# Norms at a stage's start: who builds the spreading matrix, where root's table is loaded, who splits the first weights, and in which order the first products run

## The reference

```python
def rmsnorm(x, g):
    y = xf * lax.rsqrt(jnp.mean(xf * xf, axis=-1, keepdims=True) + EPS)
    return y * g
def modulate(x, g, shift, scale):
    return rmsnorm(x, g) * (1 + scale) + shift
# first block, layers 0 and 1
a = modulate(h, norm1_g[l], sh1, sc1)          # gating MLP + differential attention, then window attention
h = h + g1 * mixer(a)
h = h + g2 * swiglu(modulate(h, norm2_g[l], sh2, sc2), ffn_w_in[l], ffn_w_out[l])
# then rmsnorm(h, final_g); second block, layers 0 and 1, with layer norms
x = layer_norm(ALPHA * x + g_m * y, ln_g[i, 0], ln_b[i, 0])
h = x * (1.0 + sc_f) + sh_f
x = layer_norm(ALPHA * x + g_f * swiglu_2(h, ...), ln_g[i, 1], ln_b[i, 1])
```

## Time and profile before

| | |
|---|---|
| runs | 4267.31 us median of 3 (4243.4 to 4297.15) |
| profiled execution | 4287.69 us, span 4285.9 us, mean granted clock 0.909 |
| TensorE | matmuls 3965.7 us (93%), 32782 |
| VectorE | 1375.1 us (32%), 2736 |
| ScalarE | 1225.9 us (29%), 2118 |
| GpSimd | 1268.8 us (30%), 669 |
| DMA | 343.5 MB, mean 80 GB/s |

### The profile page before, as it was taken

The page is one execution under the profiler, slowest core; times in us unless marked ns, Lnnn a source line. Parts: engine busy times, 40 slices in busy tenths (PEclk is TensorE's granted clock), DMA queues, the critical chain, the costliest instruction groups (busy, mean ns, idle before and its releaser), DMA issues. The chain is left out here.

```text
span 4285.9 us, 77448 instructions
## 1 busy us (share of the span) xinstructions
PE 3965.7 (93%) x32782; PEld 3303.3 (77%) x32782; DVE 1375.1 (32%) x2736; ACT 1225.9 (29%) x2118; POOL 1268.8 (30%) x669
## 2 busy tenths in 40 slices
PE   7988899999989999979699999889999989998997
PEld 5776788888777677758588988778888868766886
DVE  2327211111444211165455555432111140443112
ACT  1215211111345322232233333222111132543222
POOL 0211222222324343322122222222222222553442
PEclk6999999999999999989777677799999989998998
DMA  8210232232200434322201000113223211112222
GB/s 303 65 34 11 89 110 92 89 117 82 76 9 31 152 127 158 127 98 109 74 20 24 24 24 26 42 59 118 106 91 118 84 55 59 36 36 79 98 83 74
DMA packets 119177, 343.50 MB, mean 80 GB/s; under 512 B 34031, under 2 KB 40559, under 8 KB 118511
## 3 DMA queue, kind: packets, MB, share of 16 engines
q1 hardware_dynamic: 118895, 339.40, 23.0%
HBM read 324.55 MB, written 16.93 MB: 80 GB/s over the span
## 5 line engine op out<-in xcount | busy, mean ns | idle before, releaser
L204 POOL TENSOR_TENSOR feed_low<-ring,feed_high 128x1024 fp32r<-128x1024 f32 (+1 forms) x240 | 627.4, 2615 | 1375.7 <-ACT feed_high L197 1281.7
L221 PE MATMUL ps<-hn_high,feed_high 128*128 128x512 f32 (+1 forms) x2112 | 760.5, 360 | 24.1 <-DVE hn_low L827 13.8
L221 PE MATMUL ps<-hn_low,feed_high 128*128 128x512 f32 (+1 forms) x2112 | 753.1, 357 | 0.0
L221 PE MATMUL ps<-hn_high,feed_low 128*128 128x512 f32 (+1 forms) x2112 | 751.8, 356 | 0.0
L221 PEld LDWEIGHTS ps<-hn_high,feed_high 128*128 128x128 f32 x2112 | 402.1, 190 | 111.9 <-issue 23.4
L221 PEld LDWEIGHTS ps<-hn_high,feed_low 128*128 128x128 f32 x2112 | 401.9, 190 | 57.2
L221 PEld LDWEIGHTS ps<-hn_low,feed_high 128*128 128x128 f32 x2112 | 402.5, 191 | 54.9
L1298 DVE TENSOR_TENSOR ps<-feed_gate,ps 128x768 f32<-128x768 f32 (+1 forms) x88 | 73.0, 829 | 1009.9 <-PE ps L221 1009.1
L197 ACT ACTIVATE feed_high<-ring 128x1024 fp32r<-128x1024 f32 (+1 forms) x240 | 272.7, 1138 | 378.8 <-PE ps L221 378.8
L221 PE MATMUL ps<-feed_hid_high,feed_high 128*128 128x512 f32 (+1 forms) x1056 | 380.7, 360 | 0.0
L221 PE MATMUL ps<-feed_hid_low,feed_high 128*128 128x512 f32 (+1 forms) x1056 | 377.4, 357 | 0.0
(11 more groups left out here) (530 smaller groups left out, 7505.1 us busy)
## 6 DMA issues: line engine op xcount, KB each, us to landing
feed_side_ring<-in_ada SPq DMA_DIRECT2D x144, 512.0 KB, 5.8
ring<-in_ffn_g SPq DMA_DIRECT2D x88, 512.0 KB, 3.5
ring<-in_ffn_u SPq DMA_DIRECT2D x88, 512.0 KB, 3.5
ring<-in_ffn_d SPq DMA_DIRECT2D x64, 704.0 KB, 4.1
ring<-in_ada SPq DMA_DIRECT2D x48, 512.0 KB, 5.2
ring<-in_od_in SPq DMA_DIRECT2D x24, 512.0 KB, 3.4
ring<-in_ev_in SPq DMA_DIRECT2D x23, 512.0 KB, 4.4
ring<-in_even_in SPq DMA_DIRECT2D x20, 512.0 KB, 3.6
```

The lines of the kernel that those rows point to most:

```text
L204: pool.tensor_tensor(self.low[:, j % self.slots, 0:w], feed.ring[:, slot, 0:w], self.high[:, j % self.slots, 0:w].bitcast(F32), ALU.subtra ...
L221: mm = pe.matmul(dst, weights[a], values[b], start=first and n == 0, stop=last and n == 2)
```

## The change

`pick` is written by ScalarE with five copies, announced by a semaphore that TensorE waits for before a spread: ahead of the squares in stages with a mean, behind the root in those without. VectorE begins with the mean or the factor. Gains and shifts (`prepare`) are computed between the factor and the wait for the root. A square root of a constant is issued in the second half of the feed forward and in the output projection, one stage ahead of the norms. The low part of the first weight tile is written by VectorE, behind the root's split and before the scaling; GpSimd writes that of the second. `early_products` runs two passes for each step: high x high for all tiles as soon as the chunk's high part is there, then the two products with a low part.

```diff
--- before.py
+++ after.py
@@ -602,7 +602,6 @@
                     dve.wait_ge(turned, g - 1)
                 dve.tensor_copy(rows[:, g % 2, :], acc[:, g % 2, :]).then_inc(rows_copied, 1)
                 if g == KC:
-                    norm.sums.build(dve)
                     dve.wait_ge(sums.summed, KC)
                     norm.factor(dve)
             dve.wait_ge(turned, GROUPS)
@@ -670,16 +669,17 @@
 
     def __init__(self, k, st, tokens):
         self.k, self.n, self.q = k, tokens, tokens // 4
-        self.pick = st.sb("pick", [P, 4, P], F32R)
+        self.pick, self.picks_ready = st.sb("pick", [P, 4, P], F32R), st.sem("picks_ready")
         self.factor = st.sb("factor", [P, self.q])
         self.high, self.low = st.sb("factor_high", [P, self.q], F32R), st.sb("factor_low", [P, self.q], F32R)
 
-    def build(self, dve):
-        dve.tensor_scalar(self.pick[:, :, :], self.k.ones[:, :].unsqueeze(1).to_broadcast([P, 4, P]), 0.0, None, ALU.mult)
-        dve.drain()
+    def build(self, act):
+        act.activation(self.pick[:, :, :], self.k.ones[:, :].unsqueeze(1).to_broadcast([P, 4, P]), ACT.Copy, scale=0.0)
+        act.drain()
         for i in range(4):
             rows = slice(32 * i, 32 * i + 32)
-            dve.tensor_scalar(self.pick[rows, i, :], self.k.ones[rows, :], 1.0 / 32, None, ALU.mult)
+            ins = act.activation(self.pick[rows, i, :], self.k.ones[rows, :], ACT.Copy, scale=1.0 / 32)
+        ins.then_inc(self.picks_ready, 1)
 
     def add(self, pe, bank, values, first, last):
         return quarter_sums(self.k, pe, bank, values, self.q, first, last)
@@ -694,6 +694,7 @@
         return dve.tensor_tensor(self.low[:, :], self.factor[:, :], self.high[:, :].bitcast(F32), ALU.subtract)
 
     def spread(self, pe, dst):
+        pe.wait_ge(self.picks_ready, 1)
         for i in range(4):
             edges = [self.q * i] + [e for e in (512,) if self.q * i < e < self.q * (i + 1)] + [self.q * (i + 1)]
             for a, b in zip(edges, edges[1:]):
@@ -784,8 +785,11 @@
 
     def scalar(self, act):
         if self.offset is not None:
+            self.sums.build(act)
             self.squares(act)
         self.roots(act)
+        if self.offset is None:
+            self.sums.build(act)
 
     def roots(self, act):
         act.wait_ge(self.var_ready, 1)
@@ -850,23 +854,25 @@
         for c in range(KC):
             dve.tensor_tensor(self.k.h[:, c, 0:n], self.k.h[:, c, 0:n], self.root, ALU.add).then_inc(self.centred, 1)
 
-    def vector(self, dve):
-        if not self.rooted:
-            self.sums.build(dve)
-            if self.offset is not None:
-                self.centre(dve)
-            else:
-                self.factor(dve)
-        self.prepare(dve)
+    def vector(self, dve, weights=None):
+
         if self.offset is not None:
+            self.centre(dve)
             dve.wait_ge(self.summed, KC)
-            self.factor(dve)
+        if self.rooted:
+            self.prepare(dve)
+        else:
+            self.factor(dve, self.prepare)
+        if weights:
+            weights()
         self.apply(dve)
 
-    def factor(self, dve):
+    def factor(self, dve, meanwhile=None):
 
         sums = self.sums
         dve.tensor_scalar(sums.factor[:, :], sums.total(self.bank), 1.0 / D, EPS, ALU.mult, ALU.add).then_inc(self.var_ready, 1)
+        if meanwhile:
+            meanwhile(dve)
         dve.wait_ge(self.root_ready, 1)
         dve.reciprocal(sums.factor[:, :], sums.factor[:, :])
         sums.split(dve).then_inc(self.split_ready, 1)
@@ -938,18 +944,29 @@
 
     LAG = 2
     for step in range(KC + LAG * (len(tiles) - 1)):
-        if step < KC:
-            norm.wait(pe, step)
-        for n, (e, dst, tokens) in enumerate(tiles):
-            c = step - LAG * n
-            if not 0 <= c < KC:
-                continue
-            slot, cols = split.wait(pe, 0, e) if c == 0 else e % split.slots, slice(c * P, (c + 1) * P)
-            for a, b, _ in spans(tokens):
-                mm = split.products_of(pe, dst[:, a:b], (split.high[:, slot, cols], split.low[:, slot, cols]),
-                                       (k.hn[0][:, c, a:b], k.hn[1][:, c, a:b]), c == 0, c == KC - 1)
-            if c == KC - 1:
-                mm.then_inc(split.products, 1)
+        for low in range(2):
+            if step < KC and low:
+                norm.wait(pe, step)
+            elif step < KC:
+                pe.wait_ge(norm.high_ready, step + 1)
+            for n, (e, dst, tokens) in enumerate(tiles):
+                c = step - LAG * n
+                if not 0 <= c < KC:
+                    continue
+                if c == 0 and low:
+                    split.wait(pe, 0, e)
+                elif c == 0:
+                    pe.wait_ge(split.high_ready, e + 1)
+                slot, cols = e % split.slots, slice(c * P, (c + 1) * P)
+                for a, b, _ in spans(tokens):
+                    high, values = split.high[:, slot, cols], k.hn[0][:, c, a:b]
+                    if low:
+                        pe.matmul(dst[:, a:b], split.low[:, slot, cols], values, start=False, stop=False)
+                        mm = pe.matmul(dst[:, a:b], high, k.hn[1][:, c, a:b], start=False, stop=c == KC - 1)
+                    else:
+                        pe.matmul(dst[:, a:b], high, values, start=c == 0, stop=False)
+                if c == KC - 1 and low:
+                    mm.then_inc(split.products, 1)
 
 
 def layer_norm(k, tokens, which, bank):
@@ -979,6 +996,7 @@
 
         @st.block.scalar
         def _(act):
+            sums.build(act)
             for c in range(KC):
                 act.wait_ge(centred, c + 1)
                 if c >= 4:
@@ -992,7 +1010,6 @@
 
         @st.block.vector
         def _(dve):
-            sums.build(dve)
             dve.tensor_scalar(sums.factor[:, :], sums.total(bank), -1.0 / D, None, ALU.mult)
             sums.split(dve).then_inc(mean_split, 1)
             dve.wait_ge(mean_spread, 1)
@@ -1052,7 +1069,7 @@
 
 
     with ExitStack() as k.tmp, Stage(k, "project") as st:
-        split = Split(k, st, 2)
+        split, table = Split(k, st, 2), st.sb("table", [P, 1])
         mixed = st.sb("mixed_high", [P, KC, tokens], F32R), st.sb("mixed_low", [P, KC, tokens], F32R)
         high_ready, low_ready = st.sem("mixed_high_ready"), st.sem("mixed_low_ready")
         updated, restored = st.sem("stream_updated"), st.sem("stream_restored")
@@ -1079,6 +1096,7 @@
                 act.activation(mixed[0][:, c, :], k.mo[:, c, 0:tokens], ACT.Copy).then_inc(high_ready, 1)
                 if c == 1:
                     split.write_high(act, 0, 1)
+            act.activation(table[:, :], k.eps[:, 0:1], ACT.Sqrt)
             for n in range(KC):
                 if n + 2 < KC:
                     split.write_high(act, (n + 2) // 4, (n + 2) % 4)
@@ -1134,7 +1152,7 @@
     feed, side = k.feed, k.side
     FIRST, UP, DOWN = 2, 4 * (HALF // 2), 8
     with ExitStack() as k.tmp, Stage(k, "feed") as st:
-        split = Split(k, st, 2, SLOT)
+        split, table = Split(k, st, 2, SLOT), st.sb("table", [P, 1])
         with ExitStack() as front:
             rest, k.tmp = k.tmp, front
             norm = stream(st)
@@ -1179,7 +1197,7 @@
                     else:
                         if e == 0:
                             norm.after_split(pool)
-                        for j in range(2):
+                        for j in range(0 if e else 1, 2):
                             split.write_low(pool, 0, j, e)
                         if e == 0:
                             norm.gpsimd(pool)
@@ -1278,6 +1296,8 @@
                 feed.at = down
                 split.write_high(act, 0, 0, e2)
                 store_high(HALF - 1)
+                if h:
+                    act.activation(table[:, :], k.eps[:, 0:1], ACT.Sqrt)
                 for n in range(DOWN):
                     if n + 1 < DOWN:
                         split.write_high(act, (n + 1) // 4, (n + 1) % 4, e2)
@@ -1304,7 +1324,7 @@
 
                 feed.at, side.at = first, side_base + 2 * h
                 if h == 0:
-                    norm.vector(dve)
+                    norm.vector(dve, lambda: split.write_low(dve, 0, 0))
                     if next_c:
                         sm.products.vector(dve)
                 chunk(0, 0, 0, e)
@@ -1387,8 +1407,7 @@
             st.clear_last(pool)
             if norm:
                 norm.after_split(pool)
-                for e in range(2):
-                    split.write_low(pool, 0, e)
+                split.write_low(pool, 0, 1)
                 norm.gpsimd(pool)
             for e in range(2 if norm else 1, at):
                 split.write_low(pool, 0, e)
@@ -2239,7 +2258,6 @@
         def _(pool):
             st.clear_last(pool)
             norm.after_split(pool)
-            split.write_low(pool, 0, 0)
             split.write_low(pool, 0, 1)
             norm.gpsimd(pool)
             pool.memset(pads[0][:, :, :], 0.0)
```

## The result

The changed kernel takes **4235.6 us** (median of 19 runs, 4230.4 to 4248.6) against 4266.8 for the kernel before (19 runs, 4243.4 to 4297.2): ratio **0.9937, 95% interval 0.9921 to 0.9953**. That is 31 us of medians, where 13.5 were summed and 4254 forecast. It is 0.6%, so "same" by the forecast's line of 2%, though the interval is clear of 1. The lowest times differ by 13.0 us; over all runs on record (130 of the kernel before, 25 of the changed one) the lowest are 4238.1 and 4230.4 us, 7.8 apart. What shrank most is the scatter, from 54 to 18 us. The profiled execution took 4234.7 us with a span of 4232.9.

What follows compares the result with a forecast made beforehand. TensorE, busy 93% of the span, was taken to bound the kernel, so only its waits at normalising stages' starts could matter. Stage gains summed to 13.5 us: 4267.3 - 13.5 = 4254 us, range 4225 to 4286.

Steps and rivals of the forecast that it cites:

- Step 1: Four plain mean-square stages: matrix build leaves VectorE's path, 1.43 us won each; ScalarE's build takes 1.6, at most 0.4 lost in 512-token stages.
- Step 2: ScalarE's first-weight copies behind the matrix: no cost in wide stages, 0.25 us lost in 512-token ones; GpSimd done by about 6.3.
- Step 3 with 4: Layer-norm streams: gains and shifts in the root's wait cost 0.4 us each; root's table loaded a stage ahead wins 0.2 in three stages.
- Step 5: Four stages with a mean: VectorE takes the mean first, spread starts earlier, 0.8 us won each, between 0.3 and 1.4.
- Step 6: VectorE's first low part in the fourth feed forward no longer runs under GpSimd's weight operations: 1.0 us won; second feed forward nothing.
- Step 7: Early products, high parts first: TensorE does high products while low parts are awaited; 0.7 us per wide stage, 0.3 in 512-token feed forwards.
- The sum of waits: Gains of eight normalising stages added together: 13.5 us, 0.3%, between 6 and 22 with all bounds.
- The clock stays down: Rival: new pauses at early chunks delay the rise to 2.4 GHz; 4277 us, chance 0.13; milder form 4262, chance 0.22.
- GpSimd takes the weights first: Rival: in wide layer-norm stages GpSimd's weight split shuts out VectorE's, scaling 1.1 us late in two stages; 4256 us, chance 0.10.
- Lora's wait goes: Rival: a small shift lets VectorE's 5.30 us last-chunk operation go ahead of GpSimd, 3.4 us more won; 4251 us, chance 0.10.
- Loads come back: Rival: compiler loads root's table again at the stage, 0.2 us less in three stages, 1.3 in up to three; 4258, chance 0.05.

Runs made afterwards that it cites:

- experiment 9: Kernel before with only a delay: GpSimd does its first weight subtraction three times ahead of the recurrent stage; 4253.4 us, ratio 0.9975.
- part 1 alone: Kernel before with only the spreading matrix written by ScalarE instead of VectorE; 4245.3 us, ratio 0.9959.
- experiment 4: Changed kernel with high parts first undone, so each chunk's low products wait together with its high ones; 4248.6 us, ratio 0.9962.
- experiment 6: Kernel before with only the low part of the first weights moved from GpSimd to VectorE; 4246.0 us, ratio 0.9960.

## Why the prediction was right, and where it was short

The direction and the small size were right, the number 18 us too high. The measured time lies in the range by luck in part: the range had been widened by a scatter that I took for one of the measurement. By its steps:

- **Step 1** (matrix to ScalarE): removed as said. ScalarE's build took 1.94 us, not 1.6, for its narrow copies take 1.26 us together. In the wide stages it is still covered. In the second feed forward (below) and in lora the spread waited for it and not for the split; in the former it came 0.3 us after the split's end, inside the bound of 0.4.
```profile
1401.74 0.30 PE L702 MATMUL ps<-feed_factor_high,feed_pick 128*128 128x128 f32 x1 [3.28 <-ACT feed_pick L681]
```
- **Step 2** (copies behind it): VectorE's split ended 4.2 us after the root, before the spread (4.7); GpSimd 6.4 us after it (6.3 said). Right.
- **Step 3 with 4** (preparing, table): the loads are gone, and the inversion comes 0.91 us after the factor in the fourth feed forward against 0.88 before: the two cancel, where I had them at 0.2 lost and said 1.2 us.
```profile
3821.50 0.29 DVE L873 TENSOR_SCALAR feed_factor<-ps 128x128 f32<-128x128 f32 x1 [1.44 <-PE ps L637]
...
3822.41 0.94 DVE L877 RECIPROCAL feed_factor<-feed_factor 128x128 f32<-128x128 f32 x1
```
- **Step 5** (mean first): the spread starts 1.96 us after VectorE's first instruction against 2.45 and 2.61 before, so 0.5 to 0.65 us, not 0.8; ScalarE's longer build ends it.
```profile
3811.25 0.29 DVE L851 TENSOR_SCALAR feed_factor<-ps 128x128 f32<-128x128 f32 x1 [1.14 <-PEq L97]
...
3813.21 0.45 PE L702 MATMUL ps<-feed_factor_high,feed_pick 128*128 128x128 f32 x1 [2.61 <-ACT feed_pick L681]
```
- **Step 6** (first low part in the fourth feed forward): 1.70 to 0.75 us, as said. But the stage's end moved only 0.3 us of the 1.9 summed. Its lead of 2.8 us at the gate tile's SiLU (26.6 us after the spread of the mean, 29.4 before) is given back in the middle, with TensorE busy throughout at a granted clock of 1.00: 265 matmuls in 60 us before, 259 after. What slows them was not settled. Before, then after:
```profile
4004.00:4064.00 60.00, 60.00 (x265) 49.48 (x265) 6.64 (x9) 13.09 (x11) 26.36 (x9) 1.00 0.34 120
```
```profile
3953.00:4013.00 60.00, 60.00 (x259) 48.07 (x258) 6.65 (x9) 11.22 (x9) 26.57 (x9) 1.00 0.30 103
```
- **Step 7** (high parts first) is the mis-sized term: 0.7 and 0.3 us a stage, 4.1 together, measured 13 alone and 13 undone. Of these some 5 are waits outside lora (3.4 summed there), 1 to 4.5 lora's. The others go with more time at 2.4 GHz in the traces, which is argued, as experiment 9 has as much without this part. The sum also has 0.9 for this part in the neighbourhood projection where the step says 0.7.
- **The sum of waits.** Idle fell from 218 us (mean of two) to 199, 19 us for 13.5 summed; 3 of the surplus are lora's (5.1 for 2.1). The three parts alone took 10, 4.5 and 6 us of idle, 20.7, but this does not mean that idle adds up: 15.6 of it is lora's one wait, taken away three times. Outside lora they took 5.4, 0.6 and -0.9, together 5, and the tables 2 to 3, against 14 for all. Idle of one kernel differs by some 4 us between traces, but the first feed forward shows the reason: from the factor to the first product it is 9.52 us with part 1 alone and 10.09 with part 6 alone, 8.97 with both and part 3 (experiment 4), 8.99 before. Parts 1 and 6 each need the other, and my sum priced them as if they stood alone. Their times do not add up either (12.8, 15.7 and 15.1 against 31 to 34 for all).
- **The step that failed:** that the change "can matter only where TensorE stands still for it", and that the 54 us of scatter belonged to the measurement. The recurrent stage was entered with nothing. In the traces it gave 5 to 34 us. Rest gave 18.5; with medians 31 apart, the stage's mean share would be near 12. That is an inference and a loose one, as only profiled runs show the stage, and rest came to 3390 in experiment 9, with 3.9 of the 13 us lora's.

The rivals. *The clock stays down* did not happen: outside the three stages TensorE was busy at 1.2 GHz for 161 and 169 us, against 197 and 187 (and 167 in experiment 9). What I cited from the Trainium skill, TensorE: Matmul & The Clock Gate, "What's actually happening", that a free-running monitor lets the same code show either, agrees with the 645.0 and 674.2 us from one kernel; the monitor itself no trace shows. *GpSimd takes the weights first* did not happen in the changed kernel: in the layer-norm stages VectorE was first, by 0.16 to 0.23 us, and GpSimd's one took 3.20 to 3.27 us instead of 2.38. In experiment 6 it happened, at the price that I had given (1.1 us in a stage). *Lora's wait goes* happened, on all traces of the changed kernel: 76.5 to 71.6 us, for a reason I had not named. So the case that came true is this one, which I gave 0.10 and 4251 us (4250.4 by its own terms), and not the sum's. *Loads come back* did not happen.

## What to carry to other kernels

When a tuned kernel's runs scatter by more than the change is worth, look for the long stage whose time differs between executions of one code, and profile both kernels more than once: a local saving moves that stage's start and can win or lose several times its size. Look at the idle time that an edit removes (here it repeats within 4 us) beside the median, which also has how the clock was met. Do not add up parts that were tried alone: two can remove the same wait, and one can need another to be worth anything. Before keeping a shorter version, see that it still meets that stage well: here two versions with 193 and 197 us of idle, against 199 and 200, were 10 and 21 us slower.

## What was not expected of the hardware

- The same 13,164 matmuls took 640.0 to 674.2 us, the longer the more of it at 1.2 GHz (271 to 360 us). A delay of 2.4 us ahead of them went with 21 us more inside (one trace each).
- A 128x256 VectorE operation of 0.35 us lasted 5.30 when it started 0.03 us behind GpSimd's, through three GpSimd instructions without a gap (1.85, 1.42, 2.03), and 0.35 us when it started 0.34 us ahead. The Trainium skill, SBUF — State Buffer, "Who interferes with whom", speaks of exclusion for a whole instruction; here it lasted for three, or for one (1.96 us in experiment 9, with the clearing 0.15 us longer).
- VectorE shows pauses of 0.46 us with no releaser, whose place moves with edits ahead of them.
